# The first mixer on operands split into two rounded parts, its attention heads skewed by one, and the layer-2 modulation sums moved into the feed-forward stage

## What is computed

```python
proj = x @ w_in                                  # da q,k,v, retention q,k,v,g, memory q, three gates
y_da  = diff_attention(da_q, da_k, da_v, ...)    # 8 heads, two softmaxes each, normed with rsqrt(mean square)
y_ret = silu(r_g) * retention(r_q, r_k, r_v)     # 4 heads, group norm
m_k, m_v = split(mem @ w_mem_kv)
y_mem = memory_attention(m_q, m_k, m_v)          # 4 heads
gates = sigmoid(gate_logits + b_gate)
merged = sum over n of gates[n] * (branch[n] @ w_branch[n])
x = layer_norm(alpha * x + merged @ w_o);  x = layer_norm(alpha * x + hier_moe(x))     # 16 experts
cond = silu(c)
for l in (0, 1):
    mod = cond @ ada_w[l] + ada_b[l]             # six vectors of 1024: shifts, scales, gains
    h = x * (1 + sc_m) + sh_m;  y = even_mixer(h) or spatial_gating_mixer(h)
    x = layer_norm(alpha * x + (1 + g_m) * y)
    h = x * (1 + sc_f) + sh_f;  y = swiglu(h) if l == 0 else moe_swiglu(h)             # 8 experts
    x = layer_norm(alpha * x + (1 + g_f) * y)
```

## Time and profile before

| what | value |
|---|---|
| median of 3 runs | 2373.59 us (2372.44 to 2374.78) |
| the profiled execution's own time | 2371.91 us |
| its span, first to last instruction | 2369.9 us |
| mean granted TensorE clock | 0.981 |
| first mixer, to the end of w_o | 528.66 us |
| end of the first mixer and start of the 16-expert stage | about 561 us |
| feed-forward stage | about 1003 to 1190 us |
| 8-expert stage | about 1340 to 2335 us |

### The profile page before, as it was taken

How to read it: one execution, slowest core, us unless ns; L and a number is a source line. 1 busy time by engine, 2 the same in 40 slices (tenths; PEclk the granted TensorE clock), 3 DMA queues, 4 the chain that set the end, 5 groups by cost and what they waited for, 6 DMA issues and landing times.

```text
span 2369.9 us, 25443 instructions
## 1 busy us (share of the span) xinstructions
PE 2265.8 (96%) x10288; PEld 1855.0 (78%) x10288; DVE 1606.9 (68%) x1897; ACT 1295.6 (55%) x1560; POOL 0.4 (0%) x6
## 2 busy tenths in 40 slices
PE   8999999998999979799989899999999999999997
PEld 7668877887888866678858788888888888888886
DVE  0266233537889863345423698989898998989895
ACT  1245113106677743234320587877777787878785
POOL 0000000000000000000000000000000000000000
PEclk9999999997999999899999899999999999999999
DMA  8465455746998862045440598989999898989892
GB/s 345 187 255 214 178 209 232 274 193 242 360 356 327 330 254 107 1 178 213 161 177 1 205 388 332 372 344 352 351 351 373 330 375 326 377 325 371 333 376 100
DMA packets 51010, 638.13 MB, mean 269 GB/s; under 512 B 8640, under 2 KB 10432, under 8 KB 12096
## 3 DMA queue, kind: packets, MB, share of 16 engines
q1 hardware_dynamic: 48320, 630.34, 69.2%
q10 hardware_dynamic: 2560, 6.03, 0.7%
HBM read 635.30 MB, written 1.05 MB: 269 GB/s over the span
## 4 chain that ended last, share of the span: by engine, by line
PE 93%; DVE 3%; ACT 2%; DMA 1%; issue 1%; SPq 0%; DVEq 0%; ACTq 0%
PE psum L1678 57%; PE psum L1468 19%; PE psum L1460 5%; PE psum L1688 2%; PE psum L1562 2%; PE psum L1701 2%; PE psum L1768 2%; DMA ring<-w_branch_in 1%; PE psum L1573 1%; DMA ring<-w_in_in 0%; DVE arena L556 0%; ACT arena L543 0%; PE psum L1490 0%; PE psum L1409 0%; PE psum L1477 0%
## 5 line engine op out<-in xcount | busy, mean ns | idle before, releaser
L1325 DVE TENSOR_TENSOR stage_lo<-ring,stage_hi 128x1024 fp32r<-128x1024 f32 (+1 forms) x934 | 1108.3, 1218 | 108.4 <-ACT stage_hi L914 83.1
L914 ACT ACTIVATE stage_hi<-ring 128x1024 fp32r<-128x1024 f32 (+1 forms) x934 | 964.6, 1056 | 279.2 <-PE psum L1678 241.1
L1678 PE MATMUL psum<-stage_hi,x_hi 128*128 128x512 f32 (+1 forms) x1344 | 528.7, 393 | 14.2 <-DVE x_lo L1307 11.5
L1678 PE MATMUL psum<-stage_hi,x_lo 128*128 128x512 f32 (+1 forms) x1344 | 521.9, 388 | 0.0
L1678 PE MATMUL psum<-stage_lo,x_hi 128*128 128x512 f32 (+1 forms) x1344 | 520.6, 387 | 0.0
L1678 PEld LDWEIGHTS psum<-stage_hi,x_hi 128*128 128x128 f32 x1344 | 253.1, 188 | 63.9 <-issue 11.9
L1678 PEld LDWEIGHTS psum<-stage_hi,x_lo 128*128 128x128 f32 x1344 | 252.8, 188 | 52.9
L1678 PEld LDWEIGHTS psum<-stage_lo,x_hi 128*128 128x128 f32 x1344 | 253.4, 189 | 49.3
L1678 PE MATMUL psum<-stage_hi,h_hi 128*128 128x512 f32 x664 | 259.9, 391 | 4.4 <-DVE h_lo L1364 4.4
L1678 PE MATMUL psum<-stage_lo,h_hi 128*128 128x512 f32 x664 | 258.5, 389 | 0.0
L1468 PE MATMUL psum<-arena,ring 128*128 128x256 f32 x1024 | 226.8, 382 | 6.3 <-DVE arena L1272 4.3
(11 more groups left out here) (208 smaller groups left out, 1760.0 us busy)
## 6 DMA issues: line engine op xcount, KB each, us to landing
ring<-moe_w_gate_in SPq DMA_DIRECT2D x56, 2048.0 KB, 9.3
ring<-moe_w_up_in SPq DMA_DIRECT2D x56, 2048.0 KB, 9.5
ring<-moe_w_down_in SPq DMA_DIRECT2D x56, 2048.0 KB, 9.6
ring<-w_in SPq DMA_DIRECT2D x48, 2048.0 KB, 9.5
ring<-ada_w_in SPq DMA_DIRECT2D x15, 2048.0 KB, 8.1
ring<-w_in_in SPq DMA_DIRECT2D x14, 2048.0 KB, 10.8
mixer_tiles<-ada_w_in SPq DMA_DIRECT2D x9, 2048.0 KB, 7.8
mixer_tiles<-w_in_in SPq DMA_DIRECT2D x6, 2048.0 KB, 12.8
```

Source lines behind the costliest of these rows:

```text
L914: act.activation(chunk_view(stage_hi, f, side, p, c), chunk_source(f, side, p, c), ACT.Copy)\
L1325: dve.tensor_tensor(chunk_view(stage_lo, f, side, p, c), chunk_source(f, side, p, c), chunk_view(stage_hi, f, side, p, c).bitcast(F32), AL ...
L1678: ins = pe.matmul(dst, a, b, start=start, stop=stop)
```

## The change

In the first mixer each weight panel and each activation is split in two fp32r parts and a job is three products. The new steps `stage` (weights: ACT rounds a chunk of 128x1024 into one of HIS = 4 hi tiles, DVE writes the rest over the panel in the ring) and `split` (activations) carry this. `with_stages` puts the staging of a job ahead of the job before it, and ahead of the scores that precede that one. The hi tiles lie where the fourth and fifth slot were, so the first mixer has 3 slots. The list of steps is new: `da_turn`, `da_out` of a head stand in the next head and `da_norm` two later, with two `a_prob` tiles; r_v comes before the heads, m_q into them; in `da_norm` and `ret_var` Sqrt on ACT and the reciprocal on DVE become Ln and Exp on ACT. x and mem arrive already transposed, x is loaded again for the residual, and the router weights come in one DMA. Only the 12 ada panels of layer 1 (index 0) are summed in the first mixer. Those of layer 2 are cut into 16 pieces of 1.5 MB and loaded and summed in the feed-forward stage, one after each of its first 16 panels.

```diff
+TURNED = ("da_v", "r_v", "m_v")
+SPLIT_OF = {"branch0": "yda", "m_k": "mem", "m_v": "mem", "branch1": "yret", "branch2": "ymem", "w_o": "merged"}
+def with_stages(steps):
+    jobs = [n for n, q in enumerate(steps) if q[0] == "gemm" and not (q[1] in TURNED and q[2] % 2)]
+    at = {}
+    for before, n in zip([None] + jobs, jobs):
+        where = n if before is None else before
+        while where and steps[where - 1][0] in ("da_score", "mem_score") and steps[before][1] not in TURNED:
+            where -= 1
+        at.setdefault(where, []).append(("stage",) + steps[n][1:])
+    out = []
+    for n, q in enumerate(steps):
+        out += at.get(n, []) + [q]
+    return out
 def mixer1_steps():
-    s = [("turn_x", i, 0) for i in range(4)]
...
 def mixer1_steps():
...
+    s = splits("x", 0, 1, 2, 3) + gemms("da_q", 0, 1, 2, 3) + [("lam", 0, 0)]
+    s += gemms("da_k", 0, 1, 2, 3) + ada(0) + gemms("da_v", 0, 1, 2, 3) + ada(1)
+    s += gemms("r_v", 0, 1) + ada(2) + gemms("r_v", 2, 3) + ada(3) + splits("mem", 0, 1, 2, 3)
+    fill = [q for name, n in (("r_q", 2), ("r_k", 2), ("r_g", 4), ("gate0", 4), ("m_q", 4)) for q in gemms(name, *range(n))]
     for h in range(DA_H):
         s += [("da_score", h, 0), ("da_score", h, 1), fill.pop(0)]
...
+        if h >= 2:
+            s += [("da_norm", h - 2, 0)] + (splits("yda", h // 2 - 1) if h % 2 else [])
+        s += ([("da_turn", h - 1, 0)] if h else []) + [fill.pop(0)] + ([("da_out", h - 1, 0)] if h else [])
+    ret = lambda name, h: [("ret_" + name, h, 0)]
+    s += ret("score", 0) + gemms("m_k", 0) + [("da_norm", DA_H - 2, 0), ("da_turn", DA_H - 1, 0)]
+    s += ret("out", 0) + gemms("m_k", 1) + ada(4) + [("da_out", DA_H - 1, 0)]
+    s += ret("mean", 0) + ret("score", 1) + gemms("m_k", 2) + [("da_norm", DA_H - 1, 0)] + splits("yda", 3)
+    s += ret("var", 0) + gemms("m_k", 3) + ada(5)
+    s += ret("out", 1) + gemms("m_v", 0, 1) + ret("mean", 1) + ret("score", 2) + gemms("m_v", 2, 3) + ada(6)
+    s += ret("var", 1) + gemms("branch0", 0)
+    s += ret("out", 2) + gemms("branch0", 1) + ada(7) + ret("mean", 2) + ret("score", 3) + gemms("branch0", 2)
+    s += ret("var", 2) + gemms("branch0", 3) + ada(8)
+    s += ret("out", 3) + gemms("gate1", 0) + ret("mean", 3) + gemms("gate1", 1) + ada(9)
+    s += ret("var", 3) + gemms("gate1", 2, 3) + splits("yret", 0, 1, 2, 3)
+    s += [("mem_score", 0, 0)] + gemms("branch1", 0)
+    for h in range(1, MEM_H):
+        s += [("mem_score", h, 0)] + gemms("gate2", h - 1) + [("mem_turn", h - 1, 0)] + gemms("branch1", h)
+        s += [("mem_out", h - 1, 0)] + (ada(9 + h) if h < 3 else [])
+    s += splits("ymem", 0, 1, 2) + [("mem_turn", MEM_H - 1, 0)] + gemms("gate2", 3) + [("mem_out", MEM_H - 1, 0)]
+    s += splits("ymem", 3)
+    for i in range(4):
+        s += gemms("branch2", i) + splits("merged", i)
+    s += gemms("w_o", 0, 1, 2, 3)
...
-    return s + [("rank", 0, 0)]
+    return with_stages(s + [("rank", 0, 0)])
...
+    staged, split_at, last_use = {}, {}, {}
+    chunk_use = []
+    for q in plans[0]:
+        if q[0] == "stage":
+            staged[("gemm",) + q[1:]] = len(chunk_use)
+            turned = q[1] in TURNED
+            early = sum(1 for use in chunk_use if use[0] is w_used)
+            for n in range(3 if turned else 1):
+                chunk_use.append((w_used, early + n + 1))
+            chunk_use.append((job_done, done[("gemm", q[1], q[2] + turned)]))
+        elif q[0] == "split":
+            split_at[q[1:]] = len(split_at) + 1
+        elif q[0] == "gemm":
+            last_use[SPLIT_OF.get(q[1], "x")] = (job_done, done[q])
+    def split_name(name):
+        return SPLIT_OF.get(name, "x")
...
+    def staged_source(q, c, tensor):
+        at = panel[("gemm", q[1], q[2] - q[2] % 2)][0] * SLOT
+        wt = tensor[:, at:at + SLOT].rearrange("p (a b) -> p a b", a=KT)
+        return wt[:, 2 * c:2 * c + 2, :] if q[1] in TURNED else wt[:, :, c * P:(c + 1) * P]
+    def staged_hi(q, n):
+        wt = mixer_w_hi[n % HIS]
+        return wt.rearrange("p a b -> p (a b)").rearrange("p (a b) -> p a b", b=PANEL) if q[1] in TURNED else wt
+    def staged_chunks(q):
+        n0 = staged[("gemm",) + q[1:]]
+        return [(n0 + c, c) for c in range(4)] if q[1] in TURNED else [(n0 + m, q[2] % 2 * 2 + m) for m in range(2)]
...
-            elif s == ("da_score", 0, 0) or s[0] == "ada" and s != ("ada", 1, 11):
-                m = 0 if s[0] == "da_score" else 12 * s[1] + s[2] + 1
-                key = ("ada", m // 12, m % 12)
-                src, free = w["ada_w_2"][m // 12, m % 12], (ada_summed, m + 1)
+            elif s[0] == "ada":
+                src, free = w["ada_w_2"][s[2]], (ada_summed, s[2] + 1)
...
-        plan_loads(n, SLOTS)
+        plan_loads(n, SLOTS if n else FF_SLOTS)
...
+                if n == 1 and 0 <= k - 1 < LATES:
+                    late_load(k - 1)
+        def late_load(q):
+            if q:
+                sp.wait_ge(late_summed, q)
+            sp.dma_start(scratch(M_LATE, LATE * D), w["ada_late"][q]).then_inc(late_full, 16)
...
+        def inverse_root(tile, sums, scale, told):
+            settle(act.activation(tile, sums, ACT.Ln, bias=eps, scale=scale))
+            act.activation(tile, tile, ACT.Exp, scale=-0.5).then_inc(told, 1)
...
+                if kind == "stage":
+                    for n, c in staged_chunks(s):
+                        at, fill = panel[("gemm", a, i - i % 2)]
+                        if c == 0:
+                            act.wait_ge(slot_full[at], 16 * fill)
+                        if n >= HIS:
+                            act.wait_ge(*chunk_use[n - HIS])
+                        act.activation(staged_hi(s, n), staged_source(s, c, ring), ACT.Copy).then_inc(w_hi_set, 1)
+                    if s == ("stage", "da_q", 1):
+                        mixer_loads()
+                        act.wait_ge(cond_in, 16)
+                        act.activation(cond_row, cond_row, ACT.Silu).then_inc(cond_set, 1)
+                    continue
+                if kind == "split":
...
+                    act.activation(hi[:, 2 * i:2 * i + 2, :], from_[:, 2 * i:2 * i + 2, :], ACT.Copy)\
+                       .then_inc(in_hi_set, 1)
+                    if s == ("split", "merged", 0):
+                        act.dma_start(xT, w["x"][0]).then_inc(x_again, 16)
+                    continue
...
+        def sum_late(q):
+            dve.wait_ge(late_full, 16 * (q + 1))
+            for m in range(LATE):
+                c = 48 + LATE * q + m
+                ins = dve.tensor_tensor_reduce(late[:, m, :], late[:, m, :], cond_row, 1.0, 0.0, ALU.mult, ALU.add,
+                                               mod[:, c:c + 1])
+            ins.then_inc(late_summed, 1)
...
+                    if not f["routed"] and n % 4 == 3 and n // 4 < LATES:
+                        sum_late(n // 4)
...
+                elif kind == "stage":
+                    for n, c in staged_chunks(s):
+                        dve.wait_ge(w_hi_set, n + 1)
+                        dve.tensor_tensor(staged_source(s, c, ring_split), staged_source(s, c, ring),
+                                          staged_hi(s, n).bitcast(F32), ALU.subtract).then_inc(w_lo_set, 1)
+                elif kind == "split":
+                    from_, hi, lo = (v[:, 2 * i:2 * i + 2, :] for v in split_tiles[a])
+                    dve.wait_ge(in_hi_set, split_at[(a, i)])
+                    dve.tensor_tensor(lo, from_, hi.bitcast(F32), ALU.subtract).then_inc(in_lo_set, 1)
...
+        def split_product(s):
+            _, a, i = s
+            _, x_hi, x_lo = split_tiles[split_name(a)]
+            if a in TURNED:
+                nxt = ("gemm", a, i + 1)
+                banks = [open_bank(s), open_bank(nxt)]
+                for n, c in staged_chunks(s):
+                    pe.wait_ge(w_lo_set, n + 1)
+                    hi, lo = staged_hi(s, n), staged_source(s, c, ring_split)
+                    for t in range(TB):
+                        tokens = slice(t * P, (t + 1) * P)
+                        for k in range(2):
+                            if i == 0 and t == 0:
+                                pe.wait_ge(in_lo_set, split_at[(split_name(a), c)])
+                            for m, (wt, xt) in enumerate(((hi, x_hi), (lo, x_hi), (hi, x_lo))):
+                                ins = pe.matmul(bank(banks[t]), xt[:, 2 * c + k, tokens], wt[:, k, :],
+                                                start=(c + k + m == 0), stop=(c == 3 and k == 1 and m == 2))
+                        if c == 3:
+                            ins.then_inc(job_done, 1)
+                    if c < 3:
+                        ins.then_inc(w_used, 1)
+                return
+            b = open_bank(s)
+            for m, (n, c) in enumerate(staged_chunks(s)):
+                pe.wait_ge(w_lo_set, n + 1)
+                hi, lo = staged_hi(s, n), staged_source(s, c, ring_split)
+                for k in range(KT):
```

(15 more changed lines are left out.)

242 lines of the change are left out of this document (122 added, 120 removed).

## The result

The changed kernel takes 2384.36 us (median of 4 executions, 2384.08 to 2385.87) beside 2373.6 for the kernel before in the same runs: ratio 1.0041, interval 1.0029 to 1.0054. It is slower by 0.4%, where the forecast was 2352 and faster. The profiled execution has a span of 2382.2 us beside 2369.9.

A forecast was written before the change was run, and what follows sets the result against it. TensorE's passes were taken to bound the first mixer. The sum 80.4 - 0.5 - 19.9 - 13.1 - 18.0 - 2 - 5 gave 21.9 us less: 2350.0 profiled, said as 2352 for the median, range 2303 to 2398.

The forecast's parts named there:

- Part 1: First mixer: jobs of rounded products take 5.72 or 5.45 us instead of 6.94 or 6.87, gaining 80.4 us on TensorE.
- Part 2: Start of the mixer: transposes go, gaining 1.8 us, but the first product starts 2.3 us later; together -0.5 us.
- Part 3: First mixer: staging adds 135 us on ACT and 156 on DVE, fits beside TensorE, and costs 2.4 us of cover.
- Part 4: First mixer, three ring slots instead of five: panels landing late cost 19.9 us early and 13.1 us after the heads.
- rival in which the ring starves TensorE outright: Each of 12 ada panels in the mixer delays the next weight panel 9.1 us, 109 in all: 2428; chance 0.14.
- Part 5: Mixer heads: 15.3 us each, but 19.8 in four with Silu or Sigmoid table loads; cost 18 us.
- rival with different tables: Mixer norms: Ln and Exp need separate table loads, some 16 to 20 us of 31 uncovered: 2369; chance 0.12.
- Part 6: Feed-forward stage: loading and summing layer-2 modulation there costs 2 us, bounds 0 and 16.
- Part 7: TensorE's clock falls after idle stretches: two mixer waits of over 5 us cost 5 us.
- The likeliest: The forecast case itself: whole kernel at 2335 to 2365 us, said as 2352; chance 0.46.
- rival with the weight load: First mixer: weight loads are not hidden at 256 columns, 0.19 us more per product, 474 us: 2846; chance 0.01.
- few table loads at Ln: Sign in the mixer that the forecast is right: ACT seldom loads a table at Ln, one set serving Ln and Exp.

The follow-up runs named there:

- one_set: The changed kernel with Ln of the 12 mixer norms replaced by Identity (values come out wrong): 2369.2 us, ratio 0.9976 to the kernel before.
- warm: The changed kernel with unread whole-fp32 products placed where TensorE waits in the mixer: 2381.17 us, ratio 1.0032 to the kernel before.

## Why the prediction was wrong

**Part 1, the products: right.** 0.119 to 0.121 us in the chain where 0.119 was read; jobs of 5.7 to 6.0 us. The estimate of 0.214, worked out from what the Trainium skill (TensorE: Matmul & The Clock Gate, the sections on LDWEIGHTS and weight-path modes and, for the overlap, on packing small matmuls) states of a load's length and of which loads overlap, is met by no row of after, though each product carries its own load. The rival built on it fell. (The load of 0.19 us starts 0.11 us ahead of the start of its product, not of its end.)

**Part 2, the start: right.** The first product starts at 15.80; 15.4 was forecast.

**Part 3, staging fits beside TensorE: right as a sum.** DVE came to 302 us of 530 and ACT to 280. The forecast was 295 and 17 for DVE, and 124 and 135 for ACT, 259. What ACT's sum left out is table loads: 47 in this stretch of after, 30 before, which the 124 hold; 17 more at 1.283 are the 21 us that were missing.

**Part 4, the ring: right.** The walk gave 33.0 us for three slots. The waits for staged chunks in the trace of after, those put down to issue among them, come to 15.2 + 12.0 + 6.3 = 33.5, with 5.65 before the second r_v panel (7.5 in the walk) and 4.38 before the second gate2 panel (4.7); the 4.38 before m_v are none of the walk's, and the early waits are shorter than it had them. The size alone, on the kernel before, costs 32.1; with the sums moved as the walk says they hurt, 23.2 come back, not all of it by these waits. The load of r_q went out at 114.86 (110.1 in the walk), and its first product came at 125.37 (staged at 120.3). The rival in which the ring starves TensorE outright (2428) fell.

**Part 5, the heads: the step that failed in the mixer.** The loaded heads came at 19.1 to 20.8 us, forecast 19.8, but by two errors that cancel: with the four loads that I counted they take 17.7 to 19.4 (one_set). The heads without such a job, forecast 15.3, came at 12.3, 13.5 and 16.3. "I count no load for going between Exp and Ln" was wrong: each norm takes a load at Ln and one at Exp (L820 x12, L821 x12), and a loaded head has five and not four. Their whole price is what was bounded there, 12 norms by two loads, 31 us; it measured 20.4 (one_set), just above the 16 to 20 of the rival with different tables, to which I gave 0.12. The Silu and Sigmoid loads, counted at 18, measured 35.8 - 20.4 = 15.4. More than half of Ln's price, 11.0 us, lies behind the heads, at the last norms and those of ret, where the sum had no term for ACT at all. The sentence of the Trainium skill that I leaned on (ScalarE: Activation LUTs, Table sets), that one set holds both functions so that Ln and then Exp take one load, is not borne out by these rows: Exp, right behind Ln, takes a load of its own, so the table that serves it here is not the one that is loaded for Ln. The same page's 2.7 us (What ACT_TABLE_LOAD costs) is a load of 1283 ns, as here, and a drain of some 1380 ns behind it, which these rows don't show: where ACT waits for nothing else, the function starts within 0.02 us of the end of its load. With the forecast's assumption made true, w_o ended at 504.96, where the forecast was 504.8. That the two agree so well is luck in part. The seven steps from head to head were forecast at 4 x 19.8 + 3 x 15.3 = 125.1 us; they took 122.0 in after and 113.6 in one_set. So even with the loads at Ln the heads were 3 us shorter than forecast, and 11.5 without them. In one_set as much was lost outside the heads: 4.0 ahead of them, where r_q's first product came at 124.33 and not at 120.3, and the rest behind. The sum came out where its terms did not.

**Part 6, the late modulation: the step that failed in the feed-forward stage.** "I take 2, since six chunks of lead absorb single delays": it cost 17.1, just over the 16 of the upper bound. The round was sized well: 3.4 of sum and 6.4 to 7.2 of landing, some 10.3 us against the 9 to 11.3 forecast. What failed was holding it, and DVE's 9.4 us, each by itself against TensorE's 11.2 us a panel. The sums alone, with no landing to wait for, already cost 7.6 us. And in DVE's queue the wait for the landing keeps what is behind it, staging and the product that makes h, so a wait is added to DVE's own 9.4 us and not laid beside it; I wrote "plus its waits" and didn't price them. The lead of six chunks didn't absorb this. Loads and sums apart cost 1.6 and 7.6; tied together by a buffer of one, 17.1; untied and spread out, 1.5. Of the 17.1, 5.9 are slower products at the lower clock, a follow-on of the waits for which the sum had no term either.

**Part 7, the clock: near in size, by luck.** 5 us were counted, for two waits of over 5 us, and 5.4 came back when the time at half clock was cut from some 53 to some 21 us. That time is far more than I had thought of, and comes with many waits and not with two, but in the heads and ahead of them it lay under other waits. What the last 21 us cost wasn't tried, and the 5.9 us of the feed-forward stage were not foreseen.

**The rivals.** The likeliest was wrong by two of its terms; the time that came, 2384, is the rival with different tables (2369) and on top of it the upper bound of Part 6, a pair that I had never put together: in spans 2348.0 + 20.6 + 15.1 - 1.5 = 2382.2, with 20.4 of the 20.6 Ln's and 1.5 given back outside the two stages. That rival's price was mis-worked: its ten norms at 2.6 us are 26 us, not 16 to 20, and the loaded heads hold four norms, not six. The 2846 of the rival with the weight load adds 474 us to the kernel before and not to the forecast; it should have read 2826. Both unknowns could only lose, and each was set near its good end. What would have shown it was named, "few table loads at Ln" and "a feed-forward stage 10 us longer"; both came out on the wrong side.

## What to carry to other kernels

When a change gives work to an engine that had room, count that engine's table loads again, each by its line, over the whole stretch and not only in the loop; a pair of functions is in one table only if a row shows it without a load in between. A load, its sum and the buffer that they share make a round; where the wait for it stands in the in-order queue of an engine that also stages, add it to that engine's time, or cut it into small parts with buffers enough that a sum never waits for what it has just released. And before an idle engine's low clock is blamed, fill the waits: here taking some 32 of 53 us out of half clock gave 5.4.

## What the runs showed of the hardware

- Ln and Exp: in the changed kernel every Ln and every Exp behind it is preceded by a table load of 1283 ns, 24 in 12 norms. The timeline of ACT in one loaded head (start us, us):

```profile
186.41 1.28 ACT L873 ACT_TABLE_LOAD   x1
187.70 0.60 ACT L873 ACTIVATE mixer_tiles<-psum 128x512 f32<-128x512 f32 x1
188.32 1.28 ACT L820 ACT_TABLE_LOAD   x1
189.61 0.47 ACT L820 ACTIVATE mixer_tiles<-psum,arena 128x256 f32<-128x256 f32 x1
190.10 1.28 ACT L821 ACT_TABLE_LOAD   x1
191.40 0.42 ACT L821 ACTIVATE mixer_tiles<-mixer_tiles 128x256 f32<-128x256 f32 x1
```

- With TensorE's waits of 1 to 6 us spread over the mixer, the mean granted clock of the first 530 us was 0.95, and 0.82 between 96 and 115; before, it was 1.00. With most of these waits filled by unread products it was 0.98 (warm).
- Products of 256 columns, each with a weight load of its own, keep 0.121 us apiece over 192 in a row, four jobs long (478.46 to 501.70).
